# Which engine adds the gathered V rows of the first eight jobs: 8 and 8, or VectorE 6 and TensorE 10

## What is computed

```python
def block(xb):                                   # 128 tokens
    q = (xb @ w_query).reshape(PEER_BLOCK, PEER_HEADS, 2, half)
    ...                                          # two score lists, top 16 of each, top 16 of the 256 sums
    eidx = jnp.take_along_axis(cidx, top_pos, axis=-1)
    gate = jax.nn.softmax(top_s, axis=-1)
    act = jnp.einsum('td,thkd->thk', xb, expert_u[eidx], preferred_element_type=jnp.float32)
    coef = (gate * jax.nn.gelu(act)).astype(xb.dtype)
    return jnp.einsum('thk,thkd->td', coef, expert_v[eidx])
```

## Time and profile before

| what | value |
|---|---|
| median of 3 runs | 4041.44 us |
| the profiled execution: its time, its span | 4040.72 us, 4038.9 us |
| TensorE (PE) busy | 3164.6 us, 78% |
| VectorE (DVE) busy | 2901.7 us, 72% |
| GpSimd (POOL) busy | 2241.4 us, 55% |
| ScalarE (ACT) busy | 665.0 us, 16% |
| moved by DMA | 1458.83 MB, 361 GB/s |
| mean granted clock of TensorE | 0.885 |

### The profile page before, as it was taken

How to read it: one execution, slowest core, us unless ns; L and a number is a source line. 1 busy time by engine, 2 the same in 40 slices (tenths; PEclk the granted TensorE clock), 3 DMA queues, 4 the chain that set the end, 5 groups by cost and what they waited for, 6 DMA issues and landing times.

```text
span 4038.9 us, 35766 instructions
## 1 busy us (share of the span) xinstructions
PE 3164.6 (78%) x10390; PEld 1806.9 (45%) x10406; DVE 2901.7 (72%) x6586; ACT 665.0 (16%) x1867; POOL 2241.4 (55%) x2189
## 2 busy tenths in 40 slices
PE   5987989889988898889887776669876765566565
PEld 2575757655544455654453443335444431122222
DVE  1115565678798877678779777668677888887897
ACT  0012121221022211221102221111111110010111
POOL 0002333456566755655656566556557677777775
PEclk8988979999998899999997788879988887788988
DMA  6989979999999999999999999999999999999998
GB/s 204 280 252 327 306 267 321 355 389 396 380 381 347 362 376 366 376 397 382 401 378 372 348 356 362 361 357 371 375 365 405 404 406 409 405 401 409 408 373 318
DMA packets 670924, 1458.83 MB, mean 361 GB/s; under 512 B 53745, under 2 KB 378737, under 8 KB 670705
## 3 DMA queue, kind: packets, MB, share of 16 engines
q0 software_dynamic: 313648, 1142.49, 73.3%
q1 hardware_dynamic: 316596, 267.84, 21.3%
q10 hardware_dynamic: 40488, 46.22, 3.3%
HBM read 1422.53 MB, written 33.83 MB: 361 GB/s over the span
## 4 chain that ended last, share of the span: by engine, by line
DMA 15%; PE 9%; POOL 9%; DVE 8%; SPq 5%; issue 5%; ACT 1%; ACTq 0%; POOLq 0%; DVEq 0%
DMA peer_vring<-in_expert_v,peer_idx 9%; POOL peer_uring L863 5%; POOL peer_vring L873 4%; PE peer_psA L1251 4%; SPq L715 3%; DMA peer_uring<-in_expert_u,peer_idx 2%; DVE peer_uring L2033 2%; DMA peer_w<-keys_turned 1%; DVE peer_acc L2049 1%; PE peer_psB L1143 1%; PE peer_psB L1164 1%; DMA peer_w<-in_w_attn_o 1%; DMA peer_w<-in_w_in 1%; PE peer_psB L1036 1%; SPq L198 1%
## 5 line engine op out<-in xcount | busy, mean ns | idle before, releaser
L873 POOL DMA_INDIRECT peer_vring<-in_expert_v,peer_idx x1088 | 1116.2, 1026 | 1071.3 <-PE peer_psA L1251 789.9
L1251 PE MATMUL peer_psA<-peer_vring,peer_diag 128*128 128x512 f32 x2336 | 1291.0, 691 | 478.4 <-DMA peer_vring<-in_expert_v,peer_idx 320.4
L2033 DVE CUSTOM_DVE_ANT_0 peer_uring<-peer_uring,peer_psH 128x1024 f32<-128x1024 f32 x1088 | 1319.0, 1212 | 305.0 <-DMA peer_uring<-in_expert_u,peer_idx 299.8
L863 POOL DMA_INDIRECT peer_uring<-in_expert_u,peer_idx x1088 | 1119.5, 1029 | 503.4 <-issue 296.8
L1251 PEld LDWEIGHTS peer_psA<-peer_vring,peer_diag 128*128 128x128 f32 x2336 | 475.9, 217 | 1113.6 <-issue 938.3
L2049 DVE SCALAR_TENSOR_TENSOR peer_acc<-peer_vring,peer_coef,peer_acc 128x1024 f32<-128x1024 f32 x495 | 636.4, 1286 | 78.0 <-DMA peer_vring<-in_expert_v,peer_idx 72.1
L1220 PE MATMUL peer_psB<-peer_w,peer_hT 128*128 128x256 f32 x1152 | 280.7, 401 | 31.2 <-DMA peer_w<-in_w_query 30.5
L1036 PE MATMUL peer_psB<-peer_w,peer_hT 128*128 128x384 f32 (+1 forms) x864 | 294.5, 496 | 1.3 <-issue 0.7
L1143 PE MATMUL peer_psB<-peer_hT,peer_w 128*128 128x128 f32 (+3 forms) x1152 | 276.7, 399 | 18.4 <-DMA peer_w<-in_w_in 18.4
L1164 PE MATMUL peer_psB<-peer_hT,peer_w 128*128 128x128 f32 (+3 forms) x1024 | 255.4, 405 | 27.5 <-DMA peer_w<-in_w_attn_o 27.5
L1220 PEld LDWEIGHTS peer_psB<-peer_w,peer_hT 128*128 128x128 f32 x1152 | 232.5, 204 | 92.4 <-DMA peer_w<-in_w_query 34.9
(11 more groups left out here) (201 smaller groups left out, 2743.6 us busy)
## 6 DMA issues: line engine op xcount, KB each, us to landing
peer_w<-in_w_in SPq DMA_DIRECT2D x136, 512.0 KB, 10.7
peer_w<-in_w_in SPq DMA_DIRECT2D x24, 1536.0 KB, 15.1
peer_w<-in_w_query SPq DMA_DIRECT2D x32, 1024.0 KB, 17.2
peer_w<-in_w_ada SPq DMA_DIRECT2D x16, 1536.0 KB, 7.9
peer_uring<-in_expert_u,peer_idx POOLq DMA_INDIRECT x1088, 9.7
peer_vring<-in_expert_v,peer_idx POOLq DMA_INDIRECT x1088, 9.6
peer_w<-in_w_conv_o SPq DMA_DIRECT2D x32, 384.0 KB, 12.8
peer_w<-in_w_o SPq DMA_DIRECT2D x8, 1536.0 KB, 8.9
```

The costliest lines, as they stand in the source:

```text
L863: pool.indirect_dma_start(out=uring[:, r % U, :], out_offset=None, in_=io["expert_u"], in_offset=bass.IndirectOffsetOnAxis(ap=idx[:, s % 4 ...
L873: pool.indirect_dma_start(out=vring[:, r % V, :], out_offset=None, in_=io["expert_v"], in_offset=bass.IndirectOffsetOnAxis(ap=idx[:, s % 4 ...
L1251: last = pe.matmul(psA[:, c * 512:(c + 1) * 512], diag[:, a % DG, :], vring[:, r % V, c * 512:(c + 1) * 512], start=first, stop=False, ski ...
L2033: dve.tensor_tensor_reduce(uring[:, r % U, :], uring[:, r % U, :], psH[:], 1.0, 0.0, ALU.mult, ALU.add, act_[:, k:k + 1]).then_inc(u_used, 1)
```

## The change

`on_vector` gets a case of its own for jobs below `HEADS * T0[1]` = 8, that is for all jobs of tile 0: VectorE adds 6 rows of 16, namely 2, 5, 7, 10, 12 and 15, and TensorE the other ten: 0, 1, 3, 4, 6, 8, 9, 11, 13, 14. Nothing else is edited.

```diff
 def on_vector(s, k):
+    if s < HEADS * T0[1]:
+        return k in (2, 5, 7, 10, 12, 15)
     return k in ((1, 3, 5, 7, 9, 11, 13, 15) if s < WINDOW else (2, 5, 8, 11, 14))
```

## The result

The changed kernel takes 4063.33 us, the median of 3 runs (4058.92 to 4065.78), against 4041.44 before: a ratio of 1.0063, with an interval of 1.0044 to 1.0081. Timed a second time, six runs beside 22 of the kernel before, it came to 4059.23 against 4037.58, a ratio of 1.0044 (1.0028 to 1.0061). So it is slower: by 22 us by the medians of either timing, by 25 and 18 us by the two ratios. The profiled execution took 4063.33 us with a span of 4061.5, that is 22.6 us more span than before.

What follows compares the result with a forecast made beforehand. The prediction took TensorE's pace to bound jobs 0 to 7: 31.3 - 6.6 - 3 = 21.7 us on the profiled 4040.7 gives 4062.4, stated as 4063 us. The range leaving 2 in 10 out was 4046 to 4078.

Steps and rivals of the forecast that it cites:

- The stage: From job 0's coefficients to job 8's, iterations 1 to 8, 571.4 us before; forecast at 590 to 597 us.
- The 16 rows at the stage's mix of clocks: Rows added on TensorE in jobs 0 to 7: 27.5 us at full clock, 31.3 us with about 14% half clock.
- The waits for a diagonal: TensorE's three waits at the start of a job for ScalarE's diagonal: all should be gone, minus 6.6 us.
- The waits for w_query: TensorE's four waits for these weight blocks, 12.9 us in jobs 0 to 7: partly shortened, minus 3 us.
- Both halves alike: Iterations 1 to 4 and 5 to 8 both go at TensorE's pace, so both pay for the added rows.
- rival 2: DMA queues bound iterations 5 to 8, hiding their rows; only iterations 1 to 4 cost, about 11 us, 4052; chance 0.12.
- VectorE's relief: 16 fewer adds on VectorE in jobs 0 to 7, 20.5 us less work, counted as nothing by itself.
- The diagonals: ScalarE writes 10 per job instead of 8, 6.2 us in all; cost taken as 0, upper end 14 us.
- the V ring: The 8 slots for gathered V rows: gathers no later than before, cost nothing, within a microsecond per job either way.
- the end of the tile: gather_up of tile 0 needs job 7's last row on both engines; TensorE's lateness there is already in the sum.
- Nothing is given back later: After jobs 0 to 7 no place waits for something running by its own time, so the added time stays.
- Rival 1: Added rows keep TensorE's clock high in jobs 0 to 7: 4019 if all half clock goes; below 4044, chance 0.08.

## Why the prediction was right, step by step

The time (4063 forecast, 4063.33 and 4059.23 measured) and the direction were right. The reason was right for iterations 1 to 4 only: there TensorE sets the pace and its rows are paid for. For iterations 5 to 8 it was wrong, and the sign that the prediction gave for this, that they don't grow while 1 to 4 do, came true nearly in full: 17.4 us in iterations 1 to 4 and 2.5 us in 5 to 8 (227.2 to 229.7). By the prediction's sum each half had about 11. The first half cost more and the second less, and that the two errors cancel is luck. The stage was to take 590 to 597 us and took 591.2 and 586.9. The terms one by one:

- The 16 rows at the stage's mix of clocks, 31.3 us. The factor itself was worked out wrongly: a clock of 0.93 in the mean makes work 1/0.93 = 1.075 times as long, 29.6 us, while 1.14 holds only if 14% of the rows, not of the time, meet the half clock. TensorE's busy time in the stage grew by 23.4 us (530.4 to 553.8). L1253 alone shows 152.5 us there against 125.1 for L1251, 27.4 more, which is 16 x 1.72 at full clock. So the rows came mostly where the clock was full, and other work ran faster than before: 4.1 us of the 27.5 came back by the clock.
- The waits for a diagonal, minus 6.6 us. They are 6.6 us after as well (6.5 in the second trace): the step failed. The timelines of VectorE and TensorE in the changed kernel, at the end of iteration 6, show what the wait is:

```profile
886.69 0.56 DVE L1816 TENSOR_TENSOR peer_arena<-peer_psB,peer_rope 128x384 f32<-128x384 f32 x1 [1.61 <-issue]
...
889.94 1.28 DVE L2051 SCALAR_TENSOR_TENSOR peer_acc<-peer_vring,peer_coef,peer_acc 128x1024 f32<-128x1024 f32 x1
...
893.07 0.17 DVE L2075 TENSOR_TENSOR peer_coef<-peer_g,peer_gates 128x16 f32<-128x16 f32 x1
```

```profile
886.76 5.32 PE L1253 MATMUL peer_psA<-peer_vring,peer_diag 128*128 128x512 f32 x12
893.73 1.98 PE L1253 MATMUL peer_psA<-peer_vring,peer_diag 128*128 128x512 f32 x4 [1.65 <-ACT peer_diag L1651]
```

  VectorE takes a product that TensorE finished just ahead of its last run of rows, and needs 6.4 us from there to the coefficients; TensorE's run is three rows, 5.3 us, before and after. The moved rows stand earlier in the job, where they delay both engines alike. VectorE's load as such has no part in it: with its adds cut short the waits are 6.5 us. What the run at the end holds has: with ten rows on VectorE it is two rows in iteration 6, and the waits are 12.3 us; with four on VectorE it is six rows there, and they are 3.1 us.
- The waits for w_query, minus 3 us: 12.9 to 7.4, so minus 5.5. In the first half they are 6.2 and 7.4, in the second 6.8 and 0, and with the latter goes a stretch of half clock that no term had. In iterations 5 to 8 eight rows are 13.8 us of work at full clock; TensorE's busy time grew by 8.6 us, its idle time fell by 6.1, and 2.5 us were left.
- TensorE's idle time as a whole fell by 3.5 us (41.0 to 37.5), where I had taken 9.6 off. Too large a gain there stood against too large a cost of the rows; 31.3 - 9.6 came out near 23.4 - 3.5 = 19.9, and the rest up to 22.6 is the 1.5 and 1.3 us outside the stage. The good fit of the sum is partly chance.
- Both halves alike. I gave rival 2 (the DMA queues bound the second half) 0.12 and set its price at 11 us. It has the second half right: this costs 2.6 us in the change's profile (iterations 5 to 9) and nothing measurable when changed alone. Its mechanism is right as far as the waits for w_query go; in the change no such wait is left there, so the room was just enough and no more. What I argued against it, TensorE's few waits of 13.6 us, was weak evidence. TensorE was busy for 94% of a stretch (213.6 of 227.2 us) in which its rows were nearly free, since part of the rest was waits for weights and part of the busy time ran at half clock. What rival 2 had wrong is the first half: it took 5 us of hidden waits off there, and none are (TensorE's idle time in it grew by 2.6 us, and its busy time by 14.8). With the measured sizes it gives 14.4 + 2.6 = 17 us, close to the second measurement's ratio (18 us) and below the difference of the medians (22 us).
- VectorE's relief counted as nothing: right (ratio 1.0005). In the change its waits for TensorE grew by 23 us (119 to 142), near the 15 to 20 expected. The diagonals, the V ring and the end of the tile counted as nothing: right, since neither the pace nor the choice of rows moved the time.
- Nothing is given back later: right for the change; iterations 10 to 23 took 768.5 us (769.4 before).
- Rival 1, the clock: the mean clock of the stage rose from 0.93 to 0.94 only, far from the 0.97 that the prediction gave as a sign of being wrong. It isn't nothing, though: in iterations 5 to 8 it rose from 0.96 to 0.99, and 5.2 of the 13.8 us of added work did not show as busy time there. The sign is real. The Trainium skill, "TensorE: Matmul & The Clock Gate", section "Part 1: The HAM clock gate", says that activity is what releases the slow clock; the runs here agree, with 0.87 in iterations 1 to 4 for 12 rows fewer against 0.91, and 0.95, 0.97 and 0.99 in iterations 5 to 9 for 10, 8 and 6 rows on VectorE.

What stays open: the change in jobs 0 to 3 alone was 18 us slower in its four timed runs (4049.6 to 4061.9), but only 8.8 us in the profiled one; where the other runs lose the rest no trace shows.

## What to carry to other kernels

Before moving work from one engine to another, ask in each stretch separately who bounds it, and use the rate of the DMA for that as much as the engines' busy shares: at 392 to 395 GB/s a stretch kept its length within 3 us while TensorE's busy time went from 262 to 280 us; at 279 to 289 GB/s eight rows of 1.72 us cost 14.4 us in the mean. Then look whether the engine waits for transfers there: 6.8 us of such waits were the room, and when they were gone the next rows were paid for. A kernel can stand between two walls, so that more work costs its full price while less gains nothing; the opposite of a bad change need not be a good one. And a wait at the end of a loop can be a distance between two engines' programs (6.4 us against a run of 5.3 us here), which changes with what stands between these two points and not with the load elsewhere.

## What the runs showed that was not expected

TensorE's rows taken away were partly eaten by its clock: 12 rows, 20.6 us at full clock, left it only 4.8 us less busy, with the granted clock down from 0.91 to 0.87. A wait of 4.48 us for a weight block was followed by 16 matmuls in 6.73 us that take 3.62 otherwise. And swapping two rows between the engines (15 for 14) in 56 jobs, with the amounts untouched, cost as much as the whole change, 21 us.
